# Three-pass fp16 down products for experts of 128 columns and more, and reordered ends of the layer kernel

## The reference

```python
h = _rmsnorm(x, ln1_w[l])
proj = jnp.einsum('bsd,de->bse', h, w_in[l])          # stage A
...                                                     # recurrence, attention, w_out
x = x + jnp.einsum('bse,ed->bsd', mix, w_out[l])
x = x + _moe(_rmsnorm(x, ln2_w[l]), w_router[l], b_router[l], w_gate_up[l], b_gate_up[l],
             w_down[l], b_down[l])
# in _moe, for every block of tokens that chose expert e:
gu = x_blk @ w_gate_up[e] + b_gate_up[e]
g = jnp.minimum(gu[:, :D_EXPERT], SWIGLU_LIMIT)
u = jnp.clip(gu[:, D_EXPERT:], -SWIGLU_LIMIT, SWIGLU_LIMIT)
act = (u + 1.0) * (g * jax.nn.sigmoid(SWIGLU_ALPHA * g))
return act @ w_down[e] + b_down[e]                      # weighted by its gate, added to x
```

## Time and profile before

| what | value |
| --- | --- |
| median of 3 runs | 1908.65 us (1908.19 to 1908.91) |
| the profiled execution's own time | 1907.81 us |
| its span from the first to the last instruction | 1906.0 us |
| mean granted TensorE clock | 0.983 |
| PE busy | 1803.8 us, 95% |
| PE weight loads busy | 1662.3 us, 87% |
| DVE busy | 1366.1 us, 72% |
| ACT busy | 1193.6 us, 63% |
| POOL busy | 450.2 us, 24% |
| DMA packets | 479.05 MB, mean 251 GB/s |
| stage E's first expert matmul | at 598.74 us |

### The profile page before, as it was taken

One profiled execution on the slowest core, in us unless ns is written; L12 is line 12 of the kernel. 1 busy time (PEld: TensorE's weight loads), 2 busy tenths in 40 slices (PEclk: granted clock), 3 DMA queues, 4 the chain that ended last, 5 costly groups with the idle time before them and its releaser, 6 DMA issues.

```text
span 1906.0 us, 52979 instructions
## 1 busy us (share of the span) xinstructions
PE 1803.8 (95%) x21421; PEld 1662.3 (87%) x21421; DVE 1366.1 (72%) x2681; ACT 1193.6 (63%) x1602; POOL 450.2 (24%) x304
## 2 busy tenths in 40 slices
PE   6999998988996999999999999999999999999995
PEld 4777775666866999999999999999999999999995
DVE  4453547775358888889999999976677667767764
ACT  5576327873114677777778887755666566566563
POOL 4001000001003111122223323223233334434433
PEclk9999999999987999999999999999999999999998
DMA  4111101004439889999999999999999999999992
GB/s 151 45 44 45 34 12 56 1 1 147 151 123 354 303 298 310 307 312 325 325 319 324 313 346 319 339 325 342 363 348 361 353 364 368 374 373 367 368 374 69
DMA packets 251407, 479.05 MB, mean 251 GB/s; under 512 B 17312, under 2 KB 38096, under 8 KB 251264
## 3 DMA queue, kind: packets, MB, share of 16 engines
q1 hardware_dynamic: 231040, 443.59, 64.4%
q0 software_dynamic: 20256, 33.94, 8.2%
HBM read 466.96 MB, written 47.19 MB: 270 GB/s over the span
## 4 chain that ended last, share of the span: by engine, by line
PE 47%; issue 9%; DVE 8%; ACT 4%; DVEq 0%; ACTq 0%; POOL 0%; POOLq 0%
PE E_p_d L2157 11%; PE E_p_g L2145 4%; PE E_p_g L2148 4%; PE E_p_g L2147 4%; PE E_p_u L2148 4%; PE E_p_u L2145 4%; PE E_p_u L2147 4%; DVE E_w_lo L1956 4%; PE E_p_d L2145 3%; PE E_p_d L2148 2%; PE E_p_d L2147 2%; PE E_p_t L2120 2%; PE E_p_t L2105 2%; DVE E_up L2016 1%; ACT E_w_hi L1832 1%
## 5 line engine op out<-in xcount | busy, mean ns | idle before, releaser
L1956 DVE SCALAR_TENSOR_TENSOR E_w_lo<-E_w_st,E_w_hi 128x2048 f16<-128x2048 f32 x316 | 722.0, 2285 | 34.6 <-ACT E_w_hi L1832 32.1
L1832 ACT ACTIVATE E_w_hi<-E_w_st 128x2048 f16<-128x2048 f32 x316 | 600.7, 1906 | 46.0 <-PEq L1308 24.4
L2145 PE MATMUL E_p_g<-E_x_hi,E_w_hi 128*128 128x128 f16 (+9 forms) x2048 | 367.8, 223 | 5.7 <-DVE E_w_lo L1956 5.7
L2145 PE MATMUL E_p_u<-E_x_hi,E_w_hi 128*128 128x128 f16 (+9 forms) x2048 | 366.9, 222 | 2.5 <-DVE E_w_lo L1956 2.5
L2148 PE MATMUL E_p_g<-E_x_hi,E_w_lo 128*128 128x128 f16 (+9 forms) x2048 | 367.7, 223 | 0.0
L2147 PE MATMUL E_p_g<-E_x_lo,E_w_hi 128*128 128x128 f16 (+9 forms) x2048 | 367.7, 223 | 0.0
L2148 PE MATMUL E_p_u<-E_x_hi,E_w_lo 128*128 128x128 f16 (+9 forms) x2048 | 366.9, 222 | 0.0
L2147 PE MATMUL E_p_u<-E_x_lo,E_w_hi 128*128 128x128 f16 (+9 forms) x2048 | 366.8, 222 | 0.0
L2157 PE MATMUL E_p_d<-E_a_f,E_w_st 128*128 128x128 f32 (+3 forms) x2304 | 270.2, 276 | 9.2 <-DVE E_a_f L2026 9.2
L2157 PEld LDWEIGHTS E_p_d<-E_a_f,E_w_st 128*128 128x128 f32 x2304 | 263.3, 192 | 13.8 <-issue 7.0
L1775 POOL DMA_INDIRECT out<-E_y_rows,E_idx_out x66 | 159.2, 2412 | 478.2 <-ACT E_y_rows L1850 468.2
(11 more groups left out here) (403 smaller groups left out, 3186.7 us busy)
## 6 DMA issues: line engine op xcount, KB each, us to landing
E_w_st<-in_w_gate_up SPq DMA_DIRECT2D x130, 2048.0 KB, 10.0
E_w_st<-in_w_down SPq DMA_DIRECT2D x64, 2048.0 KB
A_w_st<-in_w_in SPq DMA_DIRECT2D x20, 512.0 KB, 3.8
A_x_rows<-in_x SPq DMA_DIRECT2D x8, 512.0 KB, 8.7
C_x_res<-in_x SPq DMA_DIRECT2D x8, 512.0 KB, 4.3
x_rows<-C_x SPq DMA_DIRECT2D x8, 512.0 KB, 5.1
out<-C_x SPq DMA_DIRECT2D x8, 512.0 KB, 5.9
h_rows<-C_h SPq DMA_DIRECT2D x8, 512.0 KB, 4.4
```

The costliest lines, as they stand in the source:

```text
L1832: act.activation(w_hi[r][:], staged(c), ACT.Copy, scale=SW).then_inc(hi_s if c < NG else down_hi_s, 1)
L1956: dve.scalar_tensor_tensor(out=w_lo[r][:], in0=staged(c), scalar=SW, in1=w_hi[r][:], op0=ALU.mult, op1=ALU.subtract, accum_out=total[:, c: ...
L2145: pe.matmul(o_, wh, hi[:, k, 0:w], start=h == 0 and k == 0, stop=False, skip_group_check=True)
```

## The change

- `HALVES` goes from 144 to 128: items of 136 and 128 columns use the three-pass form of the down products, with everything that hangs on it on ACT, DVE and SP. The wide branch on DVE takes x parts 2 and 3 only where an item has a second block of 128 tokens.
- In stage E DVE's `largest` reads 128x8 elements in place of 128x64, and `x_part` is one instruction in place of two.
- At the end of E the last two pieces of the result rows are scaled by DVE (`last_rows`) in place of ACT, and POOL no longer waits for the landing of the last scatter in E; it does so in G, at its end.
- At E's beginning PE reads the count and the borders between the transposes.
- At A's beginning `ln1` has a transfer, a transpose and a copy of its own; ACT loads the square root's table before x is there and rounds `w_hi` behind the fourth root; PE makes 24 matmuls on the identity, and `project(0, half, k)` follows each part of h as it is ready; the parameter table is turned between the halves.

```diff
-HALVES = 144
+HALVES = 128
...
+            pool.dma_start(prm_rows[0:KT, :], a.ln1_w[0].rearrange("(k p) -> k p", p=P)).then_inc(ln_in, 16)
...
+            def norms(t0):
+                squares(t0)
+                for t in range(t0 + 1, t0 + 4):
+                    squares(t)
+                    root(t - 1)
+                root(t0 + 3)
+
+            act.wait_ge(ident_s, 1)
+            act.activation(sm[:, 481:482], m.ident[:, 0:1], ACT.Sqrt)
+            norms(0)
             split_hi(0)
-            root(3)
-            act.wait_ge(prm_s, 1)
+            squares(4)
+            act.wait_ge(ln_s, 1)
             for g in range(KT):
-                if g % 2 == 0:
-                    squares(4 + g // 2)
                 h_part(g)
-                if g % 2 == 0:
+                if g % 2 == 1:
+                    if g < KT - 1:
+                        squares(4 + (g + 1) // 2)
                     root(4 + g // 2)
...
+            norms(0)
+            dve.wait_ge(ln_mm, 1)
+            dve.tensor_copy(ln1, p_in[1][:, 0, 0:KT]).then_inc(ln_s, 1)
+            dve.wait_ge(ln_s, 1)
             split_lo(0)
             for g in range(KT):
                 if g % 2 == 0:
                     mean(4 + g // 2)
                 h_part(g)
-                if g % 2 == 0:
-                    norm_row(4 + g // 2)
+                if g % 2 == 0 and g:
+                    norm_row(3 + g // 2)
+            norm_row(7)
...
             pe.wait_ge(ident_s, 1)
-            pe.wait_ge(prm_in, N_PRM)
-            pe.transpose(p_g[1][:, 1, 0:50], prm_rows[0:50, :], m.ident[0:50, 0:50]).then_inc(prm_mm, 1)
+            for _ in range(24):
+                pe.matmul(p_in[1][:, 1, 128:256], m.ident[:], m.ident[:], start=True, stop=True)
+            pe.wait_ge(ln_in, 16)
+            pe.transpose(p_in[1][:, 0, 0:KT], prm_rows[0:KT, :], m.ident[0:KT, 0:KT]).then_inc(ln_mm, 1)
...
-            for g in range(KT):
-                turn(g)
-            for k in range(KT):
-                turn(KT + k)
-                if k == 0:
+            for half in range(2):
+                for g in range(4):
+                    turn(half * KT + g)
+                if half == 0:
                     pe.wait_ge(wlo_s, 1)
-                    pe.wait_ge(h_lo_s, KT)
-                project(0, 0, k)
-            pe.wait_ge(h_lo_s, 2 * KT)
-            for k in range(KT):
-                ins = project(0, 1, k)
+                for k in range(KT):
+                    if k < 4:
+                        turn(half * KT + 4 + k)
+                    pe.wait_ge(h_lo_s, half * KT + k + 1)
+                    ins = project(0, half, k)
+                if half == 0:
+                    pe.wait_ge(prm_in, N_PRM)
+                    pe.transpose(p_in[1][:, 1, 0:50], prm_rows[0:50, :], m.ident[0:50, 0:50]).then_inc(prm_mm, 1)
...
-            def send(i):
+            def send(i, last=False):
 
-                pool.wait_ge(y_rows_s, FREE + NP * i + 2)
+                if last:
+                    pool.wait_ge(y_rows_s, FREE + NP * i)
+                    pool.wait_ge(last_rows_s, 2)
+                else:
+                    pool.wait_ge(y_rows_s, FREE + NP * i + 2)
...
-                pool.wait_ge(scattered, 16 * NB * (n_items + 1))
+                if not fast:
+                    pool.wait_ge(scattered, 16 * NB * (n_items + 1))
...
+            if not fast:
+                pool.wait_ge(m.scattered, 16 * NB * (n_sent + 1))
+                pool.sem_inc(gone_s, 1)
...
-                y_part(n_items, 2, NB)
-                y_part(n_items, 3, NB)
...
-                    dve.tensor_reduce(peak[:, c:c + 1], w_hi[r][:, :, 0:8], AX.XY, ALU.max,
+                    dve.tensor_reduce(peak[:, c:c + 1], w_hi[r][:, :, 0:1], AX.XY, ALU.max,
...
-                for h in range(2):
-                    q = 4 * (g % 2) + 2 * h
-                    r = (slice(None), slice(q, q + 2), slice(b * P, b * P + n))
-                    ins = dve.scalar_tensor_tensor(out=x_lo[r], in0=x_bank(g, first)[:, h, :].rearrange("p (b n) -> p b n", n=P)[:, :, 0:n],
-                                                   scalar=SX, in1=x_hi[r], op0=ALU.mult, op1=ALU.subtract)
-                ins.then_inc(x_lo_s, x_step(w))
+                k0 = 4 * (g % 2)
+                r = (slice(None), slice(k0, k0 + 4), slice(b * P, b * P + n))
+                dve.scalar_tensor_tensor(out=x_lo[r], in0=x_bank(g, first)[:].rearrange("p a (b n) -> p (a b) n", n=P)[:, :, 0:n],
+                                         scalar=SX, in1=x_hi[r], op0=ALU.mult, op1=ALU.subtract).then_inc(x_lo_s, x_step(w))
...
-                        x_part(i + 1, 2, w)
-                        x_part(i + 1, 3, w)
+                        for g in range(2, 2 * blocks(w)):
+                            x_part(i + 1, g, w)
...
+                def last_rows(j):
+
+                    dve.wait_ge(y_mm, NP * n_items + j - 1)
+                    dve.wait_ge(gates_s, n_items + 1)
+                    for b in range(NB):
+                        ins = dve.tensor_scalar(y_rows[:, b, j * CW:(j + 1) * CW], p_t[j % 2][:, b, :], gates[:, b:b + 1],
+                                                None, ALU.mult)
+                    ins.then_inc(last_rows_s, 1)
...
-                for g in range(NP):
-                    turn_rows(0, g, CHUNK)
+                turn_rows(0, 0, CHUNK)
+                turn_rows(0, 1, CHUNK)
                 n_items = count(pe)
                 early = early_borders(pe)
+                turn_rows(0, 2, CHUNK)
+                turn_rows(0, 3, CHUNK)
```

48 lines of the change are left out of this document (28 added, 20 removed).

## The result

The changed kernel takes **1893.91 us** (median of 5 runs, 1889.03 to 1895.87) against 1908.65 of the kernel before (5 runs, 1908.19 to 1913.11): a ratio of 0.9917, 95% interval 0.9898 to 0.9936, or 14.7 us less. Forecast were 1887.5 us (21.1 less), with a range of 1880 to 1896. The sign and the range held; a third of the forecast gain did not arrive. The profiled execution of after took 1893.33 us, 14.5 less than that of before, with a span of 1890.9.

A forecast was written before the change was run, and what follows sets the result against it. PE was taken to bound the wider items, a loop of DVE, PE and ACT legs those of 144 columns. Terms 1.6 + 2.1 + 2.1 + 2.0 + 1.9 + 7.9 + 3.5 = 21.1 us gave 1887.5 us, range 1880 to 1896.

The forecast's parts named there:

- The sample: DVE's `largest` in stage E: reading 8 elements instead of 64 saves 0.055 us each, 0.44 us for eight.
- The order in A: Stage A: projections of half 0 fill its pauses, half 1 starts about 25.0, ends 34.3 instead of 42.2: -7.9 us.
- The end: End of E: no table load, rows on DVE, POOL's drain without the wait: -3.5 us, bounds -1.3 and -4.1.
- Items of 144: Three items in stage E: smaller samples and merged `x_part` shorten DVE's loop, 123.35 to 121.8 us: -1.6 us.
- The undisturbed item of 128: Stage E, three-pass form: legs on DVE 25.2, PE's restart 0.95, ACT 11.65 us; sum 37.8 against 38.15.
- the sentence on issue gaps: Skill's 81 ns a matmul at 128 columns would make PE lose 0.7 us an item; forecast used the trace's 58 ns.
- the eight moved items: Stage E, items moved to three passes: two of 136 columns -2.1 us together, six of 128 -2.1 us together.
- the third rival: PE's 3 us pause in moved items lowers the clock, 3.4 us each, 27.3 us in all: 1914.8 us; chance 0.03.
- the five items of 112: Stage E: PE's idle 2.0 us, spent waiting for DVE, vanishes as DVE gets 0.44 us faster per item: -2.0 us.
- the moved reads: E's beginning: reads ahead of eight of 16 transposes, between -0.5 and +1.7 us, taken as 0.
- what would show it: Signs: items of 136 at 40.4, 128 at 37.8, 112 at 35.8 us; one PE wait about 3 us; `project(0)` done about 34.3.
- two rivals that did not come true: Three-pass form at 128 gives nothing or costs, 1891.6 to 1896.6 us, chance 0.23; A's beginning gives half, 1891.4, chance 0.12.

The follow-up runs named there:

- the pause filled: Changed kernel plus 32 unread bf16 identity matmuls before PE's wait for the last activated part, items of 136 and 128 columns only: 1891.83 us, ratio 0.9907.
- threshold alone: Kernel before with only HALVES put to 128 and x_part looping over the blocks an item has: 1915.50 us, ratio 1.0022.
- 12 warming matmuls: Changed kernel with 12 in place of 4 unread bf16 matmuls of 512 columns at E's beginning: 1896.07 us; with the pause filled as well, 1895.53 us.

## Why the prediction was right or wrong

**Right, and shown by a run or a row.** The sample: 0.055 us an instruction, read from two starts in the earlier trace rows, gave 8.5 us against 8.4. The order in A: half 1 started at 24.25 (forecast 25.0) and took 9.7 us (9.3), so two small errors cancel; the first turn moves with the arrival of x, from 11.7 to 12.8 us over the changed kernel and its variants. The end: -3.78 against -3.5, with the overlap of the drain at 2.6 (2.2 taken, bounds 0 and 2.8). Items of 144: -1.7 against -1.6. The undisturbed item of 128: 37.83 against 37.8, and leg by leg. These are `split_lo(4)`, PE's restart, `y_bias(0)` and the next item's `split_lo(4)` in after:

```profile
1371.97 2.29 DVE L1984 SCALAR_TENSOR_TENSOR E_w_lo<-E_w_st,E_w_hi 128x2048 f16<-128x2048 f32 x1 [0.84 <-ACT E_w_hi L1862]
1397.20 0.23 PE L2188 MATMUL E_p_d<-E_a_hi,E_w_hi 128*128 128x128 f16 x1 [2.13 <-DVE E_a_lo L2059]
1398.14 0.63 ACT L1912 ACTIVATE E_y_t<-E_p_d,E_bias 128x128 f32<-128x128 f32 x2 [0.40 <-PE E_p_d L2191]
1409.79 2.29 DVE L1984 SCALAR_TENSOR_TENSOR E_w_lo<-E_w_st,E_w_hi 128x2048 f16<-128x2048 f32 x1 [0.84 <-ACT E_w_hi L1862]
```

That is 25.23, 0.94 and 11.65 us, where 25.2, 0.95 and 11.65 were forecast. PE was busy for 34.87 against 34.5. The last number settles the sentence on issue gaps too: at about 81 ns a matmul of 128 columns, which the Trainium skill gives in "TensorE: Matmul & The Clock Gate", section "Back-to-back issue gap", PE would have been busy for 4.4 us more (192 x 23 ns) in each; the trace disagrees.

**Mis-sized: the eight moved items, 4.2 forecast and 2.6 found.** The whole difference is one term that the sum had at nothing. The falls of the clock behind PE's pause cost 1.7 us, and with the pause filled the eight take 307.5 us, 4.3 less than before. The falls were in the text as the third rival, "PE's pause costs the clock", with the right place and with 3.4 us an item where they cost 0.2 on average, since they come in some of the items only and the wait for DVE hides part.

**Mis-sized: the five items of 112, 2.0 forecast and 1.5 found.** Four of them run at 35.83, but the first, behind the moved items, takes 36.17, and PE is idle for 0.4 us in the five where it should never have been. I had multiplied one period by the count. The same edge costs 0.3 in the first item of 96. Inside the moved items the edges cancel: with the pause filled the two of 136 take 80.3 us (forecast 80.8) and the six of 128 227.2 (226.8), of which the last has 38.17.

**Missing: item 0, +3.4.** The prediction priced only the moved reads at the beginning of E, and they cost nothing. What it did not have at all is that an edit on PE moves all of PE's code behind it. The three variants of after without the standstill (12 or no identity matmuls) have item 0 at 51.36 to 51.94, the nine kernels with it at 52.47 to 55.68. About 1.5 of the 3.4 us are the standstill. The rest is the lower clock at the head of the item, 8.5 us at half speed against 3.3; whether the standstill causes that too is open, since kernels with it show 3 to 10 us of it and those without 3 to 5.

**Not settled: the stages between.** From the forget gate to E's first expert matmul the kernel before took 556.53 us, after 557.60, the eleven variants of after between 557.6 and 563.2 (the two highest have 1.6 us of this at E's beginning). Most of the difference to the kernel with the filled pause lies in one stage (B), whose window in after and in the kernel with the filled pause reads:

```profile
273.59:429.67 156.08, 132.55 (x1201) 90.08 (x1201) 112.51 (x327) 118.92 (x236) 0.00 (x0) 0.97 0.08 24
```

```profile
273.22:433.64 160.42, 138.59 (x1200) 91.91 (x1200) 112.81 (x327) 119.08 (x236) 0.00 (x0) 0.93 0.08 23
```

The same instructions, 4.3 us apart; DVE and ACT are busy for as long, and what differs in the rows is the granted clock. The kernel before does this as well (its 46 runs of the three groups lie between 1905.7 and 1914.5 us). Whether the changed beginning makes the long course more frequent, these runs cannot say; it would take profiles of many executions of one kernel.

**Also missing: 0.6 us outside the span.** Time minus span is 1.7 to 1.9 us in before and in seven of the variants (threshold alone, filled pause, 12 warming matmuls with and without it, 12 or no identity matmuls) and 2.3 to 3.6 in after and the other five. Its cause is not in the profile.

The rest agrees with "what would show it": PE stands for 3.0 us an item of 128 (forecast about 3), though in two waits for `activated_lo`, of 2.13 and 0.63 us, and not in one; the items of 152 and more, item 0 apart, did not move; ACT never waited for a transfer of weights in E. "The granted clock in stage E leaves 1.00" was named as a sign of error, and it was one.

**The range held partly by luck.** It reached to 1896 for two rivals that did not come true: an item of 128 kept its forecast length, and A gave its whole gain. What took the place of the missing gain, item 0, the stages between and the time outside the span, was in no term.
